# The first eighth of a long transformer kernel: two of eight contraction slices of the first two weight chunks in float32, and the parameter load on another queue

## What is computed

```python
h = rms_norm(x, mix_norm_g[l])                 # x: (1, 256, 1024), float32
proj = jnp.einsum('bsd,de->bse', h, w_in[l])   # w_in: (1024, 3072)
qa, ka, va, qb, kb, vb = jnp.split(proj, IN_SPLITS, axis=-1)
```

## Time and profile before

| | |
|---|---|
| median of 3 runs | 1069.42 us (1068.33 to 1071.28) |
| the profiled execution's own time | 1072.94 us |
| its span, first to last instruction | 1071.1 us |
| mean granted TensorE clock | 0.997 |
| busy: TensorE, VectorE, ScalarE | 1062.8, 833.9, 654.8 us |
| moved by DMA | 187 MB, 175 GB/s over the span |

### The profile page before, as it was taken

One profiled execution on the slowest core, in us unless ns is written; L12 is line 12 of the kernel. 1 busy time (PEld: TensorE's weight loads), 2 busy tenths in 40 slices (PEclk: granted clock), 3 DMA queues, 4 the chain that ended last, 5 costly groups with the idle time before them and its releaser, 6 DMA issues.

```text
span 1071.1 us, 20812 instructions
## 1 busy us (share of the span) xinstructions
PE 1062.8 (99%) x8144; PEld 1020.4 (95%) x8144; DVE 833.9 (78%) x1090; ACT 654.8 (61%) x942; POOL 2.7 (0%) x8
## 2 busy tenths in 40 slices
PE   9999999999999999999999999999999999999998
PEld 8888998898888999999999999999899999999998
DVE  6889876478777757888888885498998778888466
ACT  6666554456555537575787774475547587776453
POOL 0000000000000000000000000000000000000000
PEclk9999999999999999899999999999999999999999
DMA  9942463354555564533454556554332545555631
GB/s 348 244 167 80 160 234 118 119 212 154 196 188 180 187 230 158 177 130 139 177 175 178 196 172 233 195 181 158 127 125 103 198 157 196 175 188 196 230 130 73
DMA packets 30534, 186.99 MB, mean 175 GB/s; under 512 B 3735, under 2 KB 6520, under 8 KB 8840
## 3 DMA queue, kind: packets, MB, share of 16 engines
q1 hardware_dynamic: 29896, 185.05, 49.7%
q10 hardware_dynamic: 576, 1.05, 0.3%
HBM read 183.96 MB, written 1.34 MB: 173 GB/s over the span
## 4 chain that ended last, share of the span: by engine, by line
PE 96%; DMA 1%; DVE 1%; ACT 0%; issue 0%; SPq 0%; DVEq 0%
PE g L501 64%; PE d L501 31%; DMA raw<-weights 1%; PE d L504 1%; DVE w_lo L1367 1%; ACT w_hi L945 0%; DVE b_both L1367 0%; DVE a_lo L1371 0%; SPq L427 0%; DVE hy_conv L1371 0%; ACT hy_probs_t L945 0%; DVE qkv L1361 0%; DVE hy_conv L1361 0%; ACT hy_att L945 0%; DVE conv_out L1371 0%
## 5 line engine op out<-in xcount | busy, mean ns | idle before, releaser
L1367 DVE TENSOR_TENSOR w_lo<-raw,w_hi 128x2048 fp32r<-128x2048 f32 (+1 forms) x175 | 389.1, 2225 | 82.8 <-ACT w_hi L945 82.3
L945 ACT ACTIVATE w_hi<-raw 128x2048 fp32r<-128x2048 f32 (+1 forms) x174 | 324.3, 1869 | 121.1 <-PE d L501 84.5
L501 PE MATMUL g<-a_hi,w_hi 128*128 128x256 f32 x1232 | 353.7, 287 | 0.7 <-DVE w_lo L1367 0.7
L501 PE MATMUL g<-a_lo,w_hi 128*128 128x256 f32 x1232 | 349.6, 284 | 0.0
L501 PE MATMUL g<-a_hi,w_lo 128*128 128x256 f32 x1232 | 349.5, 284 | 0.0
L501 PEld LDWEIGHTS g<-a_hi,w_hi 128*128 128x128 f32 x1232 | 237.3, 193 | 4.2 <-DVE w_lo L1367 1.9
L501 PEld LDWEIGHTS g<-a_lo,w_hi 128*128 128x128 f32 x1232 | 237.4, 193 | 0.2
L501 PEld LDWEIGHTS g<-a_hi,w_lo 128*128 128x128 f32 x1232 | 237.4, 193 | 0.0
L501 PE MATMUL g<-b_both,w_hi 128*128 128x256 f32 (+1 forms) x784 | 179.9, 309 | 0.4 <-DVE b_both L1367 0.4
L501 PE MATMUL d<-hid_hi,w_hi 128*128 (+1 forms) x528 | 148.8, 282 | 0.0
L501 PE MATMUL d<-hid_lo,w_hi 128*128 (+1 forms) x528 | 148.6, 281 | 0.0
(11 more groups left out here) (302 smaller groups left out, 1327.0 us busy)
## 6 DMA issues: line engine op xcount, KB each, us to landing
raw<-weights SPq DMA_DIRECT2D x168, 1024.0 KB, 4.8
bias_tab<-bias_dram SPq DMA_DIRECT2D x8, 192.0 KB, 9.5
x<-x_t ACTq DMA_DIRECT2D x4, 256.0 KB, 5.4
raw<-weights SPq DMA_DIRECT2D x4, 256.0 KB, 6.0
raw<-weights SPq DMA_DIRECT2D x2, 512.0 KB, 7.1
mem_t<-mem_t SPq DMA_DIRECT2D x1, 1024.0 KB, 10.5
out<-x SPq DMA_DIRECT2D x3, 256.0 KB, 2.3
hy_swap<-hy_qk SPq DMA_DIRECT2D x4, 128.0 KB, 6.0
```

The source lines that it names most:

```text
L501: return pe.matmul(out, lhsT, rhs, start=start, stop=stop, skip_group_check=True)
L945: return act.activation(out, in_, func, **kw)
L1367: return dve.tensor_tensor(out, a, b, ALU.subtract)
```

## The change

Slices k = 0 and 1 of chunks 0 and 1 (a quarter of each, `RAW_K = 2`) are multiplied in float32, directly from `raw`, with a float32 copy `x_first` of x times the gain that VectorE makes. Their high and low parts aren't made. Slices 0 and 1 of x are still split, for the later chunks, but last. The load of `par` stands first in ScalarE's queue in place of SyncE's. A semaphore `raw_read` keeps chunks 3 and 4 from overwriting `raw` before TensorE has read it.

```diff
+RAW_K = 2
...
+        x_first = at("x_first", H + 32 * KB, [RAW_K, T])
...
+        OPENING = [(0, 1), (0, 2), (0, 3), (1, 1), (1, 2)]
+
+        def opening_cols(c, i):
+
+            quarter = CHUNK // 4
+            return slice(quarter, 2 * quarter) if (c, i) == (1, 1) else slice(2 * quarter, CHUNK) if c == 1 else piece(c, i)
...
                 if reused(c):
                     sp.wait_ge(lo_done, c - (U - 1))
+                if isinstance(c, int) and c in (3, 4):
+                    sp.wait_ge(raw_read, c - (U - 1))
...
-            sp.dma_start(par[:, 0:N_PARAM], io["par"][:, 0:N_PARAM]).then_inc(got_par, 16)
...
+            def opening_chunk(c, moving):
+
+                bank = G[c]
+                pe.wait_ge(piece_loaded[(0, PIECES[0] - 1)[c]], 16)
+                for k in range(KT):
+                    if k < RAW_K:
+                        if c == 0:
+                            pe.wait_ge(x_first_done, k + 1)
+                    else:
+                        if k == (6, 4)[c]:
+                            pe.wait_ge(lo_done, c + 1)
+                        elif k in ((2, 4), (2,))[c]:
+                            pe.wait_ge(piece_lo, k // 2 if c == 0 else 3)
+                        if c == 0:
+                            pe.wait_ge(x_split, count.next(x_split))
+                    for f in range(2):
+                        cols = slice(k * 2 * P + f * P, k * 2 * P + (f + 1) * P)
+                        to = bank[:, f * T:(f + 1) * T]
+                        if k < RAW_K:
+                            last = mm(to, raw[:, c, cols], x_first[:, k, :], k == 0 and f == 0, False)
+                            continue
+                        mm(to, w_hi[:, c, cols], moving[0][:, k, :], False, False)
+                        mm(to, w_hi[:, c, cols], moving[1][:, k, :], False, False)
+                        last = mm(to, w_lo[:, c, cols], moving[0][:, k, :], False, k == KT - 1)
+                    if k == RAW_K - 1:
+                        last.then_inc(raw_read, 1)
+                last.then_inc(chunk_done, 1)
...
             for j in range(W_IN_Q):
-                if j < 4:
-                    chunk("w_in", j, j % U, A, fresh=j == 0)
+                if j < 2:
+                    opening_chunk(j, A)
+                elif j < 4:
+                    if j == 2:
+                        pe.wait_ge(x_split, count.next(x_split, RAW_K))
+                    chunk("w_in", j, j % U, A)
...
+            act.dma_start(par[:, 0:N_PARAM], io["par"][:, 0:N_PARAM]).then_inc(got_par, 16)
             for i in range(KT // 2):
                 act.dma_start(x[:, 2 * i:2 * i + 2, :], io["x_t"][:, 2 * i:2 * i + 2, :]).then_inc(got_x[i], 16)
...
             act.wait_ge(got_par, 16)
-            for i in range(KT // 2):
+            act.wait_ge(got_x[0], 16)
+            for i in range(1, KT // 2):
                 act.wait_ge(got_x[i], 16)
-                hi_parts(A, 2 * i, [x[:, 2 * i + f, :] for f in range(2)], [pcol("mix_norm_g", 2 * i + f) for f in range(2)])
+                opening_hi(i)
                 piece_to_hi(0, i)
-            for i in range(PIECES[1]):
+            opening_hi(0)
+            for i in (1, 2):
                 piece_to_hi(1, i)
...
             dve.wait_ge(got_par, 16)
-            for i in range(KT // 2):
+            dve.wait_ge(got_x[0], 16)
+            for f in range(RAW_K):
+                dve.tensor_scalar(x_first[:, f, :], x[:, f, :], pcol("mix_norm_g", f), None, ALU.mult).then_inc(x_first_done, 1)
+            for i in range(1, KT // 2):
                 dve.wait_ge(got_x[i], 16)
                 prep_pair(A, "mix_norm_g", 0, x, i)
                 piece_to_lo(0, i)
-            for i in range(PIECES[1]):
+            prep_pair(A, "mix_norm_g", 0, x, 0)
+            for i in (1, 2):
                 piece_to_lo(1, i)
```

More of the change, by code:

```diff
@@ L298, in program @@
         piece_hi, piece_lo, got_table = sem("piece_hi"), sem("piece_lo"), sem("got_table")
+        x_first_done, raw_read = sem("x_first_done"), sem("raw_read")
         chunk_done, evicted = sem("chunk_done"), sem("evicted")
@@ L394, in piece @@
             return slice(i * n, (i + 1) * n)
-        def piece_count(c, i):
-            return i + 1 if c == 0 else PIECES[0] + i
+        OPENING = [(0, 1), (0, 2), (0, 3), (1, 1), (1, 2)]
+        def opening_cols(c, i):
+            quarter = CHUNK // 4
+            return slice(quarter, 2 * quarter) if (c, i) == (1, 1) else slice(2 * quarter, CHUNK) if c == 1 else piece(c, i)
         block = stack.enter_context(nc.Block())
@@ L509, in chunk @@
                 slot, bank = (FIRST[name] + jm) % U, G[(FIRST_OUT[name] + jm) % U]
-                pieces = PIECES[c] if isinstance(c, int) and c < len(PIECES) else 1
-                if pieces == 1:
-                    pe.wait_ge(lo_done, c + 1)
+                pe.wait_ge(lo_done, c + 1)
                 if reused(n):
@@ L515, in chunk @@
                 for k in range(KT):
[L516 to L519, removed]
                     if k == at_k:
@@ L1052, in piece_to_hi, with opening_hi @@
             def piece_to_hi(c, i):
-                last = i == PIECES[c] - 1
-                if last:
+                if (c, i) in ((0, 3), (1, 2)):
                     act.wait_ge(loaded[c], count.next(loaded[c], 16))
                 else:
-                    act.wait_ge(piece_loaded[piece_count(c, i) - 1], 16)
-                fn(w_hi[:, c, piece(c, i)], raw[:, c, piece(c, i)]).then_inc(hi_done if last else piece_hi, 1)
+                    act.wait_ge(piece_loaded[i if c == 0 else PIECES[0] - 1], 16)
+                cols = opening_cols(c, i)
+                fn(w_hi[:, c, cols], raw[:, c, cols]).then_inc(hi_done if (c, i) in ((0, 3), (1, 2)) else piece_hi, 1)
+            def opening_hi(i):
+                hi_parts(A, 2 * i, [x[:, 2 * i + f, :] for f in range(2)], [pcol("mix_norm_g", 2 * i + f) for f in range(2)])
             act.wait_ge(got_par, 16)
-            for i in range(KT // 2):
+            act.wait_ge(got_x[0], 16)
+            for i in range(1, KT // 2):
                 act.wait_ge(got_x[i], 16)
-                hi_parts(A, 2 * i, [x[:, 2 * i + f, :] for f in range(2)], [pcol("mix_norm_g", 2 * i + f) for f in range(2)])
+                opening_hi(i)
                 piece_to_hi(0, i)
-            for i in range(PIECES[1]):
+            opening_hi(0)
+            for i in (1, 2):
                 piece_to_hi(1, i)
@@ L1475, in piece_to_lo @@
             def piece_to_lo(c, i):
-                last = i == PIECES[c] - 1
+                last = (c, i) in ((0, 3), (1, 2))
                 if last:
@@ L1480, in piece_to_lo @@
                 else:
-                    dve.wait_ge(piece_hi, piece_count(c, i))
-                cols = piece(c, i)
+                    dve.wait_ge(piece_hi, OPENING.index((c, i)) + 1 - (c == 1))
+                cols = opening_cols(c, i)
                 sub(w_lo[:, c, cols], raw[:, c, cols], w_hi[:, c, cols].bitcast(F32)).then_inc(lo_done if last else piece_lo, 1)
```

## The result

| kernel | median us | lowest to highest | runs |
|---|---|---|---|
| before | 1069.55 | 1068.20 to 1071.28 | 12 |
| after | 1072.12 | 1070.01 to 1074.20 | 12 |

The ratio is 1.0019 (95% interval 1.0010 to 1.0028): the change makes the kernel slower by 0.19%, about 2 us. Where a few microseconds decide, the mean clock of each run has to be read too: runs at 1.000 and at 0.998 or 0.997 differ, within either kernel.

The account below looks back on a forecast made before the run. The landing of chunk 3 was taken to bound the opening, with TensorE 1.88 us idle before 28.04. TensorE's changes cancelled, and chunk 3's -0.2 us took the median 1069.42 to 1069.2, range 1067.3 to 1071.1.

Parts of the forecast that it names:

- Step 1: Raw products of chunks 0 and 1: 0.432 us per float32 product against 0.360 for three fp32r; +0.29 us a chunk, +0.58 both.
- Step 2: Start of chunk 0: the matmuls on zeros set the first real matmul, 6.7 in place of 7.24, 0.55 us earlier.
- Step 3: Rest of chunk 0: x's loads land 0 to 0.45 us later, `lo_done` 1 stays at 11.5, chunk 0 ends 0.2 earlier.
- Step 4: Chunk 1 starts 0.2 us earlier, costs 0.29 more; chunk 2 starts at about 20.15 against 20.07, so TensorE's changes cancel.
- Step 5: SyncE's queue: chunk 4 issued at 15.5, not 14.7, 0.8 us later; lands at 23.9, needed at 29.2, covered by five us.
- Step 6: Chunk 3's landing: between 0.8 us earlier and 0.4 later, taken as -0.2, which moves the end equally.
- the bounding argument: Opening to 28.04: chunk 3's landing, not TensorE, sets the transposes' start; TensorE has 1.88 us to spare, so its gains are lost.
- the slower one: Rival: chunk 3 lands later, through SyncE's wait or x's loads pushed behind `par`; 0.4 us, so 1069.8; chance 0.15.
- Slower with the clock: Rival: wait before 28.04 grows to 3 us, clock falls, +2.7 us and +0.4, so 1072.5; chance 0.05.
- The gain that gets through: Rival: ScalarE's dropped 1.34 us step brings chunk 3 about 1.3 us earlier, end at 1068.1; chance 0.15.

Follow-up runs that it names:

- with `par` back: The changed kernel with the parameter load back at the head of SyncE's queue, raw quarter kept: median 1068.73 us, ratio 1.0000.
- the repeats of before: The kernel before, unchanged, profiled a second and a third time: 1070.06 and 1070.30 us.

## Why the prediction was wrong

Forecast 1069.2 within 1067.3 to 1071.1, measured 1072.12; faster, same, slower by over 0.3% at 0.03, 0.93, 0.04, and the measured 0.19% is within "same".

- *Step 1, the price of a float32 matmul:* right. Eight records, so four products, take 1.97 and 1.99 us with their tail; the records follow each other at 0.22 us, so 0.43 per product.
- *Step 2, the start:* nearly. 6.37 instead of 6.7: the zeros took 4.75, not 5.49, and then TensorE waited 0.42 for x. With `par` back it is 5.72.
- *Step 3, the rest of chunk 0: this is the step that failed.* It put x's second and third landing "between 0 and 0.45 later" with `par` ahead, as if only the slot of issuing counted. They came 2.0 us later. The step counted the entry in the queue that gained it and said of the queue that lost it only that it "can only help". On DMA engines already full, an earlier start of the weights is taken from x. `lo_done` 1, and so chunk 3's issue, came at 13.79 instead of 11.5.
- *Step 4, chunk 2:* that the balance is near nothing was right (with `par` back chunk 2 starts at 20.51, in the repeats of before at 20.33 and 20.41), but chunk 2 started at 23.56, not at 20.15, as it inherits step 3, the idle 2.04 us and some 1.7 us lost at the lower clock.
- *Step 5, chunk 4's issue:* named rightly as later, 19.2 instead of 15.5. Its cover, five us, held: TensorE doesn't wait for chunk 4.
- *Step 6 and the bounding argument:* wrong, and wrong in itself, as it was read from one execution that ran 3.5 us above the median. I noted that distance and took it off as a constant, instead of asking where it lay. It lay in the clock near 440 us, and in the very idle time on which the argument stood. With chunk 3 at 18.9 to 19.1 there are no 1.88 us to spare, and lateness in the opening goes straight to the end. That the change stayed within 0.3% owes nothing to this argument; the lateness of the opening was simply small.
- *The rivals:* the slower one named the right place, "x's third and fourth loads pushed behind `par`", but priced it at 0.4. "Slower with the clock" had 1072.5, near the result, by another way: the fall to half pace came early in the opening, behind 2.04 us idle after the raw part, not in a grown wait before 28 us, and the median loss is there without it. The page TensorE: Matmul & The Clock Gate of the Trainium skill (Part 1) lets an idle stretch put the engine back on half clock. This trace agrees for the 2.04 us; but an idle stretch of 2.46 us in another opening and one of 2.21 us in the second execution of after brought no fall, so the length alone doesn't tell in these runs. The gain that gets through had to be ruled out by the same wrong spare time. It came to nothing for another reason: with `par` back, TensorE starts at 5.72 but then waits until 8.88 for the second weight quarter, which ScalarE takes up at 7.47.
- *Queues:* the page DMA: Bandwidth & Descriptors of the Trainium skill (Queues, rings and completion order) has the DMA engines alternating between queues. The traded landings are in keeping with it; I had used it for chunk 3 only and not for x against the weights, where it mattered.

Step 3 had also misread the rows: it put ScalarE's start on the third pair of slices at 7.71 down to the landing of x at 7.65. The trace of before, ScalarE's timeline and the chain:

```profile
7.17 0.62 ACT L945 ACTIVATE w_hi<-raw 128x512 fp32r<-128x512 f32 x1
```

```profile
2.13 6.61 DMA raw<-weights
```

By the earlier trace rows it takes 0.54 from `w_hi` to the next `a_hi`, and 7.17 + 0.54 is 7.71: ScalarE's own pace. What it waited for next was the third weight quarter, which landed at 8.74. In that execution the weights were the late ones and x was only just in time, with nothing to spare for a delay.

## What to carry over

Two queues that together fill the DMA engines share one resource: here a load moved from one to the other delayed the four loads behind it by 1.0 to 2.5 us, where its slot of issuing is 0.45, and the queue that it left got its loads 1.4 to 1.7 us earlier. Place the load on the queue whose data is needed later, or leave it. And before an argument rests on idle time in one profile, profile the kernel again: an execution that is well above its median has its excess somewhere, and it may be in the very wait that bounds the estimate.

## What the runs showed that I had not expected

- One load of 1.5 KB at the head of a queue made the four loads of 256 KB behind it land 0.5, 0.9, 1.1 and 1.5 us later; one of 56.5 KB taken from the head of the other queue, whose loads so start a slot earlier, 1.0, 2.0, 2.0 and 2.5 us.
- The same load can vary by microseconds from one execution to the next: chunk 3 took 9.30, 6.98 and 7.28 us in three executions of the kernel before, chunk 7 landed from 43.3 to 51.4 over these kernels.
- The granted clock fell to its lower level for some microseconds near 440 us, in all three profiles of the kernel before, with no idle time of TensorE in that window but matmuls of 2 and 8 columns just before it; some 60% of the timed runs of before show the lower mean clock.
- After 2.04 us idle the fall came 1.5 us behind the end of the idle time, at 11.9, and lasted to 15.3; after 2.46 us idle in the same place of another kernel there was none.
